# The first modulation in slabs of 4, 4, 4, 2, 2 tiles, and the late value products in three one-pass products

## The chip, the cores and the metric

The kernel runs on one core of a Trainium2 chip. The metric is the device time of one execution in microseconds (us), lower is better. Three runs of the kernel before gave 2869.8, 2873.56 and 2875.58 us; the median is 2873.56.

## The reference

Two transformer blocks run over one sequence of 512 tokens with 2048 features, all in float32. What matters here is how the first block begins:

```python
def first_block(x, c, norm_g, w_ada, b_ada, w_in, ...):
    cond = jax.nn.silu(c)
    mod = cond @ w_ada[l] + b_ada[l]                 # w_ada: 2048 x 6144
    shift, scale, gate = jnp.split(mod, 3, axis=-1)
    h = rms_norm(x, norm_g[l]) * (1.0 + scale[:, None, :]) + shift[:, None, :]
    z = h @ w_in[l]                                  # 2048 x 7184
    u_a, v_a, g_a, q_b, k_b, v_b, g_b, f_b = jnp.split(z, pts, axis=-1)
    y_a = chunked_spatial_gating(gelu(u_a), gelu(v_a), ln_v_g, ln_v_b, w_s, b_s) * silu(g_a)
    y_b = forgetting_attention(q_b, k_b, v_b, f_b, b_f[l]) * silu(g_b)
    ...
```

Before anything of `z` can be computed, `shift` and `scale` are needed, and these are a vector times 2048 x 4096 numbers of `w_ada` (33.5 MB). `v_a` (1024 columns) is the first product of `h`, `f_b` (the forget gates; 112 columns are taken) the second and `q_b` the third.

## The kernel before, in words

The features lie on the 128 partitions in KT = 16 tiles; `Y[:, t, :]` holds tile t of x, turned, with 512 tokens. Each engine has its own program, written out by hand; they meet in semaphores. There is no planner: the order within each program is the order of work.

**The start.** VectorE computes shift and scale in 4 slabs of 4 tiles. For a slab it goes through all 16 rows of tiles of `w_ada` (`accumulate`, L2431): a slice of 128 x (2 x 512) numbers, times the entry of c for its partition, is added to `acc`. SyncE loads these slices (L341, 512 KB each) into a ring of six, each as soon as the step that freed its place is counted in `acc_step`. TensorE then sums `acc` over the partitions (`reduce_slab`, L1689, 16 records of L1371), VectorE adds the bias and makes the columns of shift and scale (`slab_columns`, L2441 and L2443), modulates the four tiles (`slab_modulated`, L2460), and makes the low parts for later (`slab_low`, L2141, from the high parts that ScalarE makes in L1012). Before that it has multiplied the slab with the root of the norm (`slab_normed`, L2452). TensorE multiplies each modulated tile with the value weights in full float32, which takes four passes (`value_product`, L1704). These weights are loaded by GpSimd's queue (L616) into the four places of `w_raw`, each freed by `va_used`. Eight products belong to a tile: two groups of columns with four blocks of tokens each. Seven stay in their banks of PSUM over all slabs; for the eighth there is no bank, so after each slab VectorE adds it to a parked sum (`park`, L2475 and L2477) and its bank, number 7, also takes the sums of `reduce_slab`. TensorE does the sums of the next slab three products before the end of the present one.

**Behind it.** The groups f, q, k, v and so on (`GROUPS`) run in split precision: weights and operand are each cut in a high part (`w_hi` by ScalarE, L714 and L739; `op_hi`) and a low part (`w_lo` by VectorE, L2004; `op_lo`), and three one-pass products replace the four passes: high x high (L1414), low operand x high (L1417), high x low weights (L1420). `w_hi` and `w_lo` have four places, freed by `w_used`; the raw weights have four places of two tiles, freed by `lo_done`, and SyncE loads them (L383). f's tiles are 112 columns wide. While VectorE is free of the slabs it accumulates the next part of the modulation (`part_tile`, L2027); its loads for f's part are in L358.

**SyncE's order** after the slabs is: the f part of `w_ada`, b_f, the spill of x (L363, 4 MB from `Y` to HBM), b_s (L540), the eight weight pairs of f, the two rows ln_v_g and ln_v_b (L564), q's weights mixed with `a_raw`, the next part of `w_ada`. **ScalarE's order** is: the first two narrow high parts of f and two more, Gelu on the first four banks (L1032), Gelu on three banks and on the parked sum (L1035, L1037), then f's other high parts.

Of the kernel before, what the change touches and what calls it, by code (L numbers as in the profile page):

```python
# [5 lines left out]
P = 128  # L6
# [24 lines left out]
def plan():  # L31
# [36 lines left out]
    kc = 0  # L68
# [122 lines left out]
START_RING, SLABS, SLAB = 6, 4, 4  # L191
# [92 lines left out]
def va_block(b):  # L284

    slab, m = divmod(b, 4)
    return m % 2, SLAB * slab + 2 * (m // 2)


def value_order(slab):  # L290


    return (0, 1, 2, 3) if slab < SLABS - 1 else (0, 2, 1, 3)


# [29 lines left out]
def sync_program(B, sp):  # L325
# [24 lines left out]
    for m in range(KT // 2):  # L350
        n = SLABS * KT + m
        if m < START_RING:

            sp.wait_ge(sem("acc_step"), n - START_RING + 1)
        else:

            sp.wait_ge(sem("part_tile"), 2 * (m - START_RING) + 2)
# [4 lines left out]
    sp.wait_ge(sem("x_turned"), KT)  # L362
    sp.dma_start(B.x_sp, B.Y[:, :, :]).then_inc(sem("spilled"), 16)  # L363

    def weights(n, m, r=0):
# [3 lines left out]
        if g["kc"] + 2 * m < 2 * RAW:  # L369

            sp.wait_ge(sem("va_used"), 4 * (SLABS - 1) + value_order(SLABS - 1).index(m) + 1)
        if g["kc"] + 2 * m >= 2 * RAW:

            sp.wait_ge(sem("lo_done"), r * 8 + (g["kc"] + 2 * m - 2 * RAW + 2))
# [146 lines left out]
    def conv_loads(i, m):  # L521
# [7 lines left out]
        if 0 <= j < 8:  # L529
            if j >= CONV_SLOTS:  # L530
# [75 lines left out]

def pool_program(B, pool):
# [3 lines left out]
    for b in range(4 * SLABS):  # L611
        g, kt = va_block(b)
        if b >= RAW:
# [4 lines left out]
            .then_inc(B.va_in[b % RAW], 16)  # L618

# [80 lines left out]
def scalar_program(B, act):  # L700
# [5 lines left out]
    def high_tile(c, width):  # L706
        raw, fill = c // 2 % RAW, c // (2 * RAW)
        if c % 2 == 0:

            act.wait_ge(B.w_in[raw], 16 * (fill + 1))  # L710
# [1281 lines left out]
def vector_program(B, dve):  # L1992
# [519 lines left out]
    for t in range(SLAB):  # L2512
        slab_low(SLABS - 1, t)
# [496 lines left out]
```

## Time and profile before

| | |
|---|---|
| profiled execution | 2875.39 us, its span 2873.6 us |
| median of three runs | 2873.56 us |
| TensorE busy | 2788.6 us, 97% |
| VectorE busy | 1791.1 us, 62% |
| ScalarE busy | 1045.0 us, 36% |
| GpSimd busy | 43.1 us, 1% |
| DMA | 451.32 MB, 157 GB/s over the span |
| mean granted TensorE clock | 0.995 |

The span goes from the first to the last instruction; the time of the execution is 1.8 us longer. All times in what follows are microseconds from the span's start. A clock of 1.00 means that TensorE was granted its full 2.4 GHz throughout, and at the lower level it has 1.2 GHz. In the page's 40 slices of 71.8 us the DMA engines are at least 90% busy in the first two (digit 9), with 348 and 358 GB/s, and 60 to 70% in the next two, with 212 and 213 GB/s.

### The profile page before, as it was taken

How to read it: one execution, taken by the hardware profiler on the slowest of the kernel's cores; microseconds unless marked ns; L12 is line 12 of the kernel's file. 1: busy time of each engine (PE TensorE's matmuls, PEld its weight loads, DVE VectorE, ACT ScalarE, POOL GpSimd, SP SyncE). 2: the span in 40 equal slices, each digit the busy share in tenths (PEclk: the TensorE clock that was granted, in tenths of full speed). 3: DMA queues.
4: the chain of work that ended last, by engine and by line, in shares of the span. 5: the costliest groups of instructions: out<-in, count | busy, mean ns of one | idle time of the engine just before them, and what ended most of it. 6: DMA issues, size and time to landing. Idle time of an engine off the chain costs nothing.

```text
span 2873.6 us, 35430 instructions
## 1 busy us (share of the span) xinstructions
PE 2788.6 (97%) x12484; PEld 2203.0 (77%) x12484; DVE 1791.1 (62%) x2754; ACT 1045.0 (36%) x1636; POOL 43.1 (1%) x51
## 2 busy tenths in 40 slices
PE   7999999999999988999999999999999999999999
PEld 4468887777788866888877777777788688888887
DVE  6855675555598767445565647383977777525454
ACT  3032222444332365332243535443322542224233
POOL 0000000000000000000000000000000000100000
PEclk9999999999999999999999999999999999999999
DMA  9966553222356647465522223224667265333332
GB/s 348 358 212 213 190 191 95 75 74 80 120 191 220 237 145 234 151 216 192 189 89 81 82 87 102 73 88 141 217 228 220 89 234 191 106 99 96 124 111 96
DMA packets 239242, 451.32 MB, mean 157 GB/s; under 512 B 23918, under 2 KB 45888, under 8 KB 234482
## 3 DMA queue, kind: packets, MB, share of 16 engines
q1 hardware_dynamic: 236288, 440.85, 46.7%
q0 software_dynamic: 2304, 8.39, 0.8%
q8 instruction: 87, 1.43, 0.2%
q14 instruction: 59, 0.48, 0.1%
q10 hardware_dynamic: 504, 0.17, 0.0%
HBM read 422.06 MB, written 27.30 MB: 156 GB/s over the span
## 4 chain that ended last, share of the span: by engine, by line
PE 83%; DVE 6%; ACT 4%; issue 3%; DVEq 2%; DMA 1%; ACTq 1%; SPq 0%
PE ps L1414 20%; PE ps L1420 20%; PE ps L1417 19%; PE ps L1704 4%; PE ps L1433 2%; PE ps L1430 2%; PE ps L1427 2%; PE ps L1862 1%; PE ps L1853 1%; PE ps L1384 1%; PE ps L1981 1%; PE ps L1978 1%; PE ps L1389 1%; PE ps L1386 1%; PE ps L1352 1%
## 5 line engine op out<-in xcount | busy, mean ns | idle before, releaser
L2004 DVE TENSOR_TENSOR w_lo<-w_raw,w_hi 128x512 fp32r<-128x512 f32 (+2 forms) x672 | 448.7, 674 | 547.7 <-ACT w_hi L714 302.7
L1414 PE MATMUL ps<-op_hi,w_hi 128*128 128x512 f32 (+2 forms) x2800 | 779.3, 397 | 9.0 <-ACT w_hi L714 5.0
L1420 PE MATMUL ps<-op_hi,w_lo 128*128 128x512 f32 (+2 forms) x2800 | 755.3, 389 | 9.2 <-DVE w_lo L2004 4.7
L1417 PE MATMUL ps<-op_lo,w_hi 128*128 128x512 f32 (+2 forms) x2800 | 754.9, 389 | 0.6 <-DVE op_lo L2141 0.6
L1420 PEld LDWEIGHTS ps<-op_hi,w_lo 128*128 128x128 f32 (+1 forms) x2800 | 524.3, 188 | 123.5 <-DVE w_lo L2769 7.2
L1414 PEld LDWEIGHTS ps<-op_hi,w_hi 128*128 128x128 f32 (+1 forms) x2800 | 516.9, 188 | 125.7 <-issue 10.1
L1417 PEld LDWEIGHTS ps<-op_lo,w_hi 128*128 128x128 f32 (+1 forms) x2800 | 525.9, 188 | 112.7 <-DVE op_lo L2141 1.4
L714 ACT ACTIVATE w_hi<-w_raw 128x512 fp32r<-128x512 f32 (+2 forms) x416 | 242.7, 592 | 601.2 <-PE ps L1420 442.3
L739 ACT ACTIVATE w_hi<-w_raw 128x512 fp32r<-128x512 f32 x288 | 181.8, 632 | 583.6 <-PE ps L1420 454.1
L2027 DVE SCALAR_TENSOR_TENSOR acc<-a_raw,vec,acc 128x512 f32<-128x512 f32 x525 | 382.0, 747 | 16.2 <-DMA a_raw<-in_w_ada 13.6
L2769 DVE TENSOR_TENSOR w_lo<-w_raw,w_hi 128x512 fp32r<-128x512 f32 x128 | 83.6, 686 | 60.7 <-ACT w_hi L1270 55.3
L1427 PE MATMUL ps<-w_hi,op_hi 128*128 128x512 f32 x384 | 111.9, 400 | 5.3 <-ACT w_hi L714 4.4
L1433 PE MATMUL ps<-w_lo,op_hi 128*128 128x512 f32 x384 | 109.3, 393 | 3.5 <-DVE w_lo L2004 3.3
L1704 PE MATMUL ps<-w_raw,arena 128*128 128x512 f32 x256 | 111.7, 597 | 0.0
L1430 PE MATMUL ps<-w_hi,op_lo 128*128 128x512 f32 x384 | 108.9, 392 | 0.0
L1704 PEld LDWEIGHTS ps<-w_raw,arena 128*128 128x128 f32 x256 | 48.8, 192 | 61.0 <-issue 59.3
L2693 DVE TENSOR_TENSOR w_lo<-w_raw,w_hi 128x512 fp32r<-128x512 f32 x64 | 44.3, 692 | 76.3 <-ACT w_hi L1170 76.3
L1307 ACT ACTIVATE arena<-arena 128x2048 f32<-128x2048 f32 (+1 forms) x32 | 54.1, 1702 | 100.3 <-DVE arena L2825 100.3
L1427 PEld LDWEIGHTS ps<-w_hi,op_hi 128*128 128x128 f32 x384 | 71.5, 189 | 23.1 <-ACT w_hi L714 5.7
L1433 PEld LDWEIGHTS ps<-w_lo,op_hi 128*128 128x128 f32 x384 | 72.0, 189 | 21.4 <-DVE w_lo L2004 6.5
L1270 ACT ACTIVATE w_hi<-w_raw 128x512 fp32r<-128x512 f32 x128 | 74.8, 620 | 33.0 <-PE ps L1420 33.0
L1430 PEld LDWEIGHTS ps<-w_hi,op_lo 128*128 128x128 f32 x384 | 72.5, 189 | 15.5
(314 smaller groups left out, 2461.3 us busy)
## 6 DMA issues: line engine op xcount, KB each, us to landing
a_raw<-in_w_ada SPq DMA_DIRECT2D x216, 512.0 KB, 4.0
w_raw<-in_w_in_e SPq DMA_DIRECT2D x160, 512.0 KB, 4.7
w_raw<-in_w_in SPq DMA_DIRECT2D x96, 512.0 KB, 4.7
arena<-in_w_ada SPq DMA_DIRECT2D x72, 512.0 KB, 6.6
w_raw<-in_w_in_o SPq DMA_DIRECT2D x64, 512.0 KB, 4.4
w_raw<-in_w_out SPq DMA_DIRECT2D x32, 512.0 KB, 4.9
w_raw<-in_w_out_e SPq DMA_DIRECT2D x32, 512.0 KB, 5.0
w_raw<-in_w_out_o SPq DMA_DIRECT2D x32, 512.0 KB, 3.8
```

Of the source, the lines that this page charges most:

```text
L714: Act(B.w_hi[:, c % RING, 0:width], B.w_raw[:, raw, c % 2, 0:width], ACT.Copy).then_inc(sem("hi_done"), 1)
L739: Act(B.w_hi[:, t % RING, 0:width], B.w_raw[:, raw, t % 2, 0:width], ACT.Copy).then_inc(sem("hi_done"), 1)
L1414: mm(ps[0:m, bank + j, 0:tok], hi[:, cols], B.op_hi[:, k, 0:tok], start=first, stop=False)
L1417: mm(ps[0:m, bank + j, 0:tok], hi[:, j * P:j * P + m], B.op_lo[:, k, 0:tok], start=False, stop=False)
L1420: last = mm(ps[0:m, bank + j, 0:tok], lo[:, j * P:j * P + m], B.op_hi[:, k, 0:tok], start=False, stop=last_t)
L1427: mm(ps[:, bank + j, :], B.op_hi[:, k, rows], hi, start=first, stop=False)
L1430: mm(ps[:, bank + j, :], B.op_lo[:, k, j * P:j * P + P], hi, start=False, stop=False)
L1433: last = mm(ps[:, bank + j, :], B.op_hi[:, k, j * P:j * P + P], lo, start=False, stop=last_t)
L1704: return mm(ps[:, 4 * g + j, :], slab_input(B, slab)[:, t % SLAB, j * P:(j + 1) * P], B.w_raw[:, b % RAW, k, :], start=t % SLAB == 0 if ow ...
L2004: V.tensor_tensor(B.w_lo[:, c % RING, 0:width], B.w_raw[:, c // 2 % RAW, c % 2, 0:width], B.w_hi[:, c % RING, 0:width].bitcast(f32), ALU.s ...
L2027: last = V.scalar_tensor_tensor(out=sums, in0=x, scalar=col, in1=sums, op0=ALU.mult, op1=ALU.add)
L2769: V.tensor_tensor(B.w_lo[:, c % RING, :], B.w_raw[:, c // 2 % RAW, c % 2, :], B.w_hi[:, c % RING, :].bitcast(mybir.dt.float32), ALU.subtract)\
```

## The change

- `w_ada` is taken in 5 slabs of 4, 4, 4, 2 and 2 tiles. There are 80 accumulation steps instead of 64; the last 32 are half as wide. A load of the narrow slabs brings two rows of tiles into one place of the ring, in two DMAs of 256 KB.
- ScalarE instead of VectorE modulates the tiles (Identity with scale and bias) and makes the high parts of the operand beside it.
- The value products of the first two slabs stay as they were. From slab 2 on (`SPLIT_SLAB`) they are done as three one-pass products. ScalarE makes the high parts of the value weights and issues their loads (`value_high`, `value_load`), and GpSimd makes the low parts (`value_low`, a subtraction of 128 x 512 numbers, 16 of them).
- From slab 2 on the sums of the next slab stand directly behind the parked block's products of the last pair.
- VectorE normalises the next slab before it parks the last, and its low parts come one step earlier. The park of the last slab and the first two low parts of f's weights are put between the steps of f's part.
- The spill of x is issued by ScalarE's queue after the value activations. b_s is loaded behind f's weights. f's weights count on from the value products in the same rings.

The core of the diff:

```diff
-START_RING, SLABS, SLAB = 6, 4, 4
+START_RING, SLABS = 6, 5
+SLAB_AT, SLAB_TILES = (0, 4, 8, 12, 14), (4, 4, 4, 2, 2)
+SPLIT_SLAB = 2
...
+        for k in range(rows):
+            sp.dma_start(start_slot(B, n)[:, k, :, :], w_ada[:, kt + k, 0:2, first:first + width])\
+                .then_inc(B.start_in[n % START_RING], 16)
...
-    sp.wait_ge(sem("x_turned"), KT)
-    sp.dma_start(B.x_sp, B.Y[:, :, :]).then_inc(sem("spilled"), 16)
...
         if name == "f":
+            sp.wait_ge(sem("acc_step"), SLABS * KT)
+            sp.dma_start(at(AT_BS, 1, HEADS_A * P)[:, 0, :],
+                         A["b_s"].rearrange("o h t -> o (h t)").to_broadcast([P, HEADS_A * P])).then_inc(sem("bs_in"), 16)
             sp.wait_ge(sem("op_tile"), KT)
-            sp.wait_ge(sem("va_used"), 4 * SLABS)
+            sp.wait_ge(sem("w_used"), KT)
...
+def value_low(B, pool, b):
+    for c in (2 * (b - SPLIT_BLOCK), 2 * (b - SPLIT_BLOCK) + 1):
+        pool.wait_ge(B.sem("hi_done"), c + 1)
+        if c >= RING:
+            pool.wait_ge(B.sem("w_used"), c - RING + 1)
+        B.nc.gpsimd.tensor_tensor(B.w_lo[:, c % RING, :], B.w_raw[:, b % RAW, c % 2, :],
+                                  B.w_hi[:, c % RING, :].bitcast(mybir.dt.float32), mybir.AluOpType.subtract)
+        B.nc.gpsimd.drain().then_inc(B.sem("lo_done"), 1)
...
+        act.wait_ge(sem("columns_or_parked"), 2 * slab + 1)
+        for t in range(SLAB_TILES[slab]):
+            k = SLAB_AT[slab] + t
+            x, scale, bias = slab_input(B, slab)[:, t, :], B.mod[:, 16 + k:17 + k], B.mod[:, k:k + 1]
+            if slab >= SPLIT_SLAB:
+                Act(B.op_hi[:, k, :], x, ACT.Identity, scale=scale, bias=bias).then_inc(sem("op_high"), 1)
+                nc.scalar.drain()
+            Act(x, x, ACT.Identity, scale=scale, bias=bias).then_inc(sem("modulated"), 1)
...
+            if slab == SPLIT_SLAB:
+                value_load(SPLIT_BLOCK + RAW - 1)
+            for c in range(max(split, RING), split + 2 * SLAB_TILES[slab]):
+                if c % 2 == 0 and SPLIT_BLOCK + RAW + (c - RING) // 2 < KT:
+                    value_load(SPLIT_BLOCK + RAW + (c - RING) // 2)
+                value_high(c)
...
+                act.wait_ge(sem("columns_or_parked"), 2 * SLABS)
                 Act(va[:, 3, :], at(AT_PARK, S), ACT.Gelu).then_inc(B.bank_free[1], 1)
+                act.wait_ge(sem("x_turned"), KT)
+                act.dma_start(B.x_sp, B.Y[:, :, :]).then_inc(sem("spilled"), 16)
...
+    def split_products(slab, b, k, blocks):
+        g, kt = VA_BLOCKS[b]
+        t, c = kt + k, 2 * (b - SPLIT_BLOCK) + k
...
+        for j in blocks:
+            bank, first, last = value_bank(slab, g, t, j)
+            mm(bank, B.op_hi[:, t, rows(j)], hi, start=first, stop=False)
+        pe.wait_ge(sem("lo_done"), c + 1)
+        for j in blocks:
+            mm(value_bank(slab, g, t, j)[0], B.op_hi[:, t, rows(j)], lo, start=False, stop=False)
+        pe.wait_ge(sem("op_tile"), t + 1)
+        for j in blocks:
+            bank, first, last = value_bank(slab, g, t, j)
+            done = mm(bank, B.op_lo[:, t, rows(j)], hi, start=False, stop=last)
+        return done
...
     slab_columns(SLABS - 1)
-    slab_modulated(SLABS - 1)
-    for t in range(SLAB):
-        slab_low(SLABS - 1, t)
-
     for t in range(KT):
         part_tile(FIRST["f"], t)
-    park(SLABS - 1)
+        if t < SLAB_TILES[SLABS - 1]:
+            slab_low(SLABS - 1, t)
+        if t == 9:
+            park(SLABS - 1)
+        if t in (9, 11):
+            if t == 9:
+                dve.wait_ge(sem("lo_done"), KT)
+            low_tile(KT + (t - 9) // 2, GROUPS[FIRST["f"]]["width"])
```

## Rows read from the trace of the kernel before

**Rows 1.** Chain of waits over the start: start, length, engine, tile, line, records.
```profile
110.27 1.68 PE ps L1371 x16
111.95 27.57 PE ps L1704 x64
141.20 30.15 PE ps L1704 x70
...
176.19 7.79 DMA w_raw<-in_w_in
...
184.68 1.20 PE ps L1414 x4
185.88 0.91 PE ps L1417 x4
```

**Rows 2.** TensorE in order of time: start, length; idle before it at the end.
```profile
170.79 0.80 PE L1414 MATMUL ps<-op_hi,w_hi 128*112 128x512 f32 x1
...
182.20 1.02 PE L1358 MATMUL ps<-const 128*128 128x512 f32 x2
```

**Rows 3.** VectorE in order of time, one slab's end and f's part.
```profile
121.72 1.28 DVE L2431 SCALAR_TENSOR_TENSOR acc<-arena,vec,acc 128x1024 f32<-128x1024 f32 x1
122.91 0.69 DVE L2141 TENSOR_TENSOR op_lo<-arena,op_hi 128x512 fp32r<-128x512 f32 x1
...
125.31 11.00 DVE L2431 SCALAR_TENSOR_TENSOR acc<-arena,vec,acc 128x1024 f32<-128x1024 f32 x8
136.98 0.69 DVE L2477 TENSOR_TENSOR arena<-arena,ps 128x512 f32<-128x512 f32 x1 [0.67 <-PE ps L1704]
137.86 2.29 DVE L2452 TENSOR_TENSOR arena<-Y,arena 128x2048 f32<-128x2048 f32 x1 [0.19 <-issue]
...
146.56 12.72 DVE L2027 SCALAR_TENSOR_TENSOR acc<-arena,vec,acc 128x512 f32<-128x512 f32 x15
```

**Rows 4.** ScalarE in order of time: high parts of a slab, value activations.
```profile
142.31 2.19 ACT L1012 ACTIVATE op_hi<-arena 128x512 fp32r<-128x512 f32 x4 [26.02 <-DVE arena L2460]
...
171.39 1.45 ACT L1035 ACTIVATE arena<-ps 128x1536 f32<-128x1536 f32 x1 [0.75 <-PE ps L1704]
172.74 0.62 ACT L1037 ACTIVATE arena<-arena 128x512 f32<-128x512 f32 x1
```

**Rows 5.** GpSimd in order of time, late in the kernel.
```profile
2467.08 1.90 POOL L659 CAST gain_rows<-arena 128x2048 fp32r<-128x2048 f32 x1 [387.29 <-DVE Y L2940]
...
2474.99 4.61 POOL L663 TENSOR_TENSOR gain_rows<-arena,gain_rows 128x2048 fp32r<-128x2048 f32 x1
```

**Rows 6.** VectorE in order of time, the same stretch.
```profile
2467.17 2.34 DVE L2004 TENSOR_TENSOR w_lo<-w_raw,w_hi 128x512 fp32r<-128x512 f32 x1 [0.23 <-ACT w_hi L739]
...
2475.82 4.92 DVE L2004 TENSOR_TENSOR w_lo<-w_raw,w_hi 128x512 fp32r<-128x512 f32 x2 [0.73 <-ACT w_hi L739]
```

**Rows 7.** Busy time by stretch: length, PE, PEld, DVE, ACT, POOL, clock, DMA, GB/s.
```profile
26.40:28.60 2.20, 0.02 (x1) 0.00 (x0) 1.99 (x3) 2.20 (x3) 0.06 (x1) 1.00 1.04 386
28.60:32.00 3.40, 3.36 (x5) 1.48 (x6) 3.19 (x3) 1.78 (x1) 2.30 (x3) 0.64 1.05 387
32.00:36.00 4.00, 4.00 (x9) 1.66 (x8) 3.90 (x4) 1.86 (x1) 0.00 (x0) 0.88 1.04 390
```

**Rows 8.** DMA from 155 to 161 us, all packets.
```profile
DMA packets 80, 2.62 MB, mean 437 GB/s; under 512 B 0, under 2 KB 0, under 8 KB 0
```

**Rows 9.** DMA queues from 8 to 9 us: packets, MB, share of 16 engines.
```profile
q1 hardware_dynamic: 49, 0.40, 97.6%
q10 hardware_dynamic: 47, 0.02, 7.2%
```

**Rows 10.** DMA issues from 130 to 215 us: count, KB each, median to landing.
```profile
w_raw<-in_w_in SPq DMA_DIRECT2D x8, 112.0 KB, 2.4
...
arena<-in_ln_v_b SPq DMA_DIRECT2D x1, 512.0 KB, 5.8
```

**Rows 11.** SyncE's queue in order of time: start, length of the issue.
```profile
175.71 0.43 SPq L564 DMA_DIRECT2D arena<-in_ln_v_b  x1
```

More of the change, by code:

```diff
@@ L618, in pool_program @@
             .then_inc(B.va_in[b % RAW], 16)
+    for b in range(SPLIT_BLOCK, KT):
+        value_low(B, pool, b)
     queries = at(AT_QST, 2, S)
@@ L1692, in reduce_slab @@
         if slab:
-            pe.wait_ge(sem("parked"), slab)
+            pe.wait_ge(sem("columns_or_parked"), 2 * slab)
         else:
             pe.wait_ge(sem("variance"), 1)
-        reduce_parts(slab % 2, ps[:, 7, :]).then_inc(sem("start_summed"), 1)
+        tiles = SLAB_TILES[slab]
+        for v in range(2):
+            for j in range(tiles):
+                last = mm(ps[:, 7, tiles * v + j:tiles * v + j + 1], B.acc[:, slab % 2, v, j * P:(j + 1) * P],
+                          B.ones[:, 0:1], start=True, stop=True)
@@ L1698, in value_product, with value_bank @@
+        last.then_inc(sem("start_summed"), 1)
+    def value_bank(slab, g, t, j):
+        own = g == 1 and j == 3
+        first, last = (SLAB_AT[slab], SLAB_AT[slab] + SLAB_TILES[slab] - 1) if own else (0, KT - 1)
+        return ps[:, 4 * g + j, :], t == first, t == last
     def value_product(slab, b, k, j):
-        g, kt = va_block(b)
+        g, kt = VA_BLOCKS[b]
+        t = kt + k
         pe.wait_ge(B.va_in[b % RAW], 16 * (b // RAW + 1))
-        t = kt + k
-        own = g == 1 and j == 3
@@ L1704, in value_product @@
-        return mm(ps[:, 4 * g + j, :], slab_input(B, slab)[:, t % SLAB, j * P:(j + 1) * P],
-                  B.w_raw[:, b % RAW, k, :], start=t % SLAB == 0 if own else t == 0,
-                  stop=t % SLAB == SLAB - 1 if own else t == KT - 1)
+        pe.wait_ge(sem("modulated"), t + 1)
+        bank, first, last = value_bank(slab, g, t, j)
+        return mm(bank, slab_input(B, slab)[:, t - SLAB_AT[slab], j * P:(j + 1) * P],
+                  B.w_raw[:, b % RAW, k, :], start=first, stop=last)
@@ new lines, in split_products @@
+    def split_products(slab, b, k, blocks):
+        g, kt = VA_BLOCKS[b]
+        t, c = kt + k, 2 * (b - SPLIT_BLOCK) + k
+        hi, lo = B.w_hi[:, c % RING, :], B.w_lo[:, c % RING, :]
+        rows = lambda j: slice(j * P, (j + 1) * P)
+        pe.wait_ge(sem("hi_done"), c + 1)
+        pe.wait_ge(sem("op_high"), t + 1)
+        for j in blocks:
[6 more added lines that the diff above has]
+        for j in blocks:
+            bank, first, last = value_bank(slab, g, t, j)
+            done = mm(bank, B.op_lo[:, t, rows(j)], hi, start=False, stop=last)
+        return done
@@ L2527, in vector_program @@
     y_tile = lambda t: Y[:, t, :]
-    for c in range(4):
+    for c in (KT + 2, KT + 3):
         low_tile(c, GROUPS[FIRST["f"]]["width"])
```

188 lines of the change are left out of this document (113 added, 75 removed).

## The prediction

> **What bounds the kernel now.** I read the share of each engine first, then the chain of waits over the start, then TensorE, VectorE, ScalarE and SyncE in order of time there, then the transfers. TensorE is busy 97% of the span, so a change at the start is worth exactly what it moves TensorE's first product of q. The chain [rows 1] is TensorE alone through the value products: a wide slab is 32 four-pass products (64 records, two each) in 27.57 us, 0.862 us a product, and 1.68 us of sums, a period of 29.25. It ends with 30.15 us of products from 141.20, so the value products end at 171.35; I call this end V. Then 16 narrow tiles of f run from 170.8 to 182.2 [rows 2], one filling product 1 us long ends near 183.2, and q's first product starts at 184.68, because q's first weights, issued at 176.19, landed 7.79 us later [rows 1]. So q0 stands on a transfer, with V 13.3 us behind it. VectorE is the second limit: a chained 1024-wide accumulation costs 11.00/8 = 1.37 us, one with a short operation between 1.19, a low part 0.60, the normalising 2.29, a park 0.69, a chained 512-wide one 12.72/15 = 0.85 [rows 3].
>
> **Slabs 0 and 1.** The modulation leaves VectorE for ScalarE at 0.55 us a tile [rows 4], against 0.5 on VectorE, behind one semaphore. TensorE always has 3 products (2.6 us) left behind the sums, which hide it (without them it would be some 0.7 us a slab). Slab 2 starts as before: 111.95 + 3 x 0.862 = 114.5.
>
> **Three passes.** A one-pass product is 0.91/4 = 0.227 us [rows 1], three are 0.68 in place of 0.862. The 64 products of slabs 2 to 4 take 43.5 in place of 55.1 us: 11.6 less on TensorE if nothing is late; a k-tile is 2.72, slab 2 is 21.8, a narrow slab 10.9. Slab 2's park sum is done after 6.25 tiles' work, at 114.5 + 17.7 = 132.2. One more sum (5 slabs, narrow ones half of 1.68) adds nothing: 3 x 1.68 becomes 2 x 1.68 + 2 x 0.84.
>
> **VectorE, now 80 steps.** The last 32 are half as wide, but at 0.85 chained they cost 27.1 where 16 wide ones cost 22. In slab 3's loop, from the columns at 112.5: 10 x 0.85 + 4 x 0.67 + 4 x 0.60 = 13.6, and the two-tile normalising 1.2, done at 127.3: 4.9 us before the park sum at 132.2. Park, sums and columns follow: sums 133.1 to 134.0, columns 134.7. Slab 4's loop: 12 x 0.85 + 2 x 0.67 + 2 x 0.60 = 12.7, to 147.4, normalising 1.2, park 0.7: 149.4. TensorE had slab 3's park sum at 145.6 and now waits in order in front of the sums (in before it had 3 products there). So TensorE would idle 3.9 us, sum, do 18 passes (4.1), start slab 4 at 154.5 and end it 10.9 later: V = 165.4, 6.0 earlier, not 11.6.
>
> **The low parts on GpSimd.** No row shows this operation 512 wide beside an accumulation. The 2048-wide one takes 4.61 us [rows 5], so 1.15 for a quarter; the bounds are 0.69 (VectorE's time for it, [rows 3]) and 1.9 (a whole 2048-wide cast, [rows 5]). I take 1.15. TensorE has 2.72 us a tile, so by itself it is hidden. But what runs beside it pays: VectorE's subtraction of two SBUF tiles, 0.69 alone, took 2.34 and two took 4.92 while GpSimd worked [rows 5, 6]; the first waited until GpSimd was done (2467.08 + 1.90 = 2468.98, + 0.5 = 2469.5) and so did the other (2479.60). The accumulation too reads two SBUF tiles. Each GpSimd low part then holds VectorE for 1.15 less the gap of 0.15 between its instructions: 1.0 us (bounds 0, if accumulation does not collide, and 1.9). The first eight fall in VectorE's slack: four in slab 3's loop, which has 4.9 us, four in slab 2's, which has the 1.83 that the modulation leaves and its own waits (0.67 before the park, [rows 3]). If that cover were gone, each would cost 1.0 more. Four fall in slab 4's loop, which is on the path: + 4.0. The wait of GpSimd itself for VectorE delays TensorE's second passes by about 0.7 in slab 3 and 0.5 in slab 4. So: park 153.7, TensorE idle 146.2 to 153.8, sums to 154.7, 18 passes to 158.8, slab 4 with its waits 11.5: V = 170.3.
>
> **Clock.** After the 2.2 us idle at 26.4 the granted clock of the next 3.4 us was 0.64 [rows 7], that is 2.4 us at the lower level of 1.2 GHz; together with the 0.88 of the slice behind, 3.4 us, a loss of 1.7. With 7.6 us idle I charge 1.7 (bounds 0 and 3.5): V = 172.0, 0.7 later than before.
>
> **f.** Four accumulations more of the f part fall behind four further GpSimd low parts: VectorE is through its 16 f steps, park and two early low parts at about 175.6. The third narrow low part is ready at 175.9, where TensorE wants it at 173.8; f's fifth tile starts at 177.0 and f could end at 185.2.
>
> **The spill, now on ScalarE's queue.** It is issued after the value activations, 1.45 + 0.62 [rows 4] and a high part behind V: 174.7. In before it sat at 150, in front of f's weights on SP's own queue, under 20 us of TensorE work. Its cost there was nothing. It moves as 32 KB packets: 80 packets, 2.62 MB, at 437 GB/s [rows 8], so 9.7 us for 4.19 MB, 8 packets on each of 16 engines, 1.2 us each. How two queues share an engine stands in [rows 9]: in one microsecond q1 moved 49 packets of x and q10 47 of the small rows, one for one, while q1 had 97.6% of the time. So while the spill runs, SP's queue gets some 8 packets an engine. f's loads (256 rows of 448 bytes, 16 an engine) take 2.4 us alone [rows 10]; the last three pairs are issued at 176.2, 176.8 and 177.6, inside the spill (176.0 to 185.8), and land behind it. Their rest takes some 2.2 us: 188.0. Behind them in the same queue now stand b_s (moved here), both ln rows, and then q0. In before f's last pair landed near 177.1, the second ln row at 175.71 + 5.8 = 181.5 [rows 10, 11], so 2.2 a row, and q0 another 2.5 later, at 184.0. So three rows are 6.6: 194.6, and q0 197.1. With the high part of 0.7 TensorE starts q at 197.8.
>
> The Trainium skill has another rule here. "DMA: Bandwidth & Descriptors", section on queues, rings and completion order, says that an engine changes rings only at packet ends and that a packet typically holds 9 to 17 descriptors; by that f's loads would need one or two turns and lose about 2 us, which leads to the rival of a fair share below. Rows 9 speak against it.
>
> **Sum.** q starts at 197.8 in place of 184.7: + 13.1. TensorE was idle before it for over 5 us, so another clock loss of 1.7 (bounds 0 and 1.7): + 14.8; I take + 14.7, since the filling product covers a little. After q's first tile the work is the same and TensorE-bound, so it is not given back. Against the profiled execution's 2875.39 (span 2873.6 and 1.8 around) this is 2890.1. That execution is 1.8 above the median of 2873.56, so the forecast is 2888.
>
> **Rivals.** (1) Fair share: collision as above, but the queues share by bytes. SP's 2.4 MB (f's rest, b_s, ln, q0) at half of 400 GB/s take 12 us from 177, + 2: q0 at 191, q at 191.7, + 7.0: 2880.6. For: rows 9 have packets of 8 KB against small ones, no row has 32 KB beside another queue; against: the count there is one for one. (2) No collision on VectorE: V = 165.4, spill issued at 167.7, through at 178.8, f's rest 181, b_s and ln 187.6, q0 190.1, q 190.8, clock 1.7: + 7.8, 2881.4. Against it stand rows 5 and 6, which are of subtractions; for it, that no row has an accumulation there. (3) Not slower: TensorE's saved passes decide. No collision, V = 165.4, f ends 176.9, and SP's loads are not held up. q0, issued at 171.4 behind three broadcast rows, lands 3 x 2.2 + 2.5 = 9.1 us after f's last pair (169.7 + 2.4): 181.2, q 181.9, - 2.8: 2870.8; with the spill shared by bytes 183.7, - 1: 2872.5; with all cover 177.9, - 6.8: 2866.8. The point from which it decides: q0 lands before 184.0. (4) The narrow loads don't deliver: 1 KB rows halve the rate and slab 4's loop waits for data. 12 steps are in the ring, so 2 of 8 loads could be late, 3 us: this only widens the upper end.
>
> **Chances.** Forecast 0.58, rival 1 0.17, rival 2 0.11, rival 3 0.14. A measurement of this kernel tells 0.2%, 5.7 us, from no change (2867.8 to 2879.3). Faster: a third to a half of rival 3, 0.06. Same: the rest of it, and the lower part of 1 and 2 (spread 3 us), 0.15. Slower: 0.79. Range: rivals 1 and 2 lie inside; of rival 3 the milder half; above, GpSimd at 1.4 instead of 1.15 on 8 steps (2 us), the late loads (3) and a third clock drop (1.7): 2873 to 2896. The likeliest one's own range is 2882 to 2896.
>
> **What would show it.** Collision: accumulations in slab 4's loop near 1.9 us where GpSimd is busy, four of them or more; without it 0.75 at most. TensorE: idle before slab 4's sums, 7.6 us (3.9 without collision). V: 172 (165.4). Spill: f's last three pairs land about 10 us after issue in place of 2.4, TensorE idle within f, and q's first weights land 25 us after V, not 13. The forecast is wrong if q starts before 190; its mechanism is wrong if V comes before 168 or if f runs through without a wait.

## The result, and the profile after

The changed kernel takes 2886.7 us (median of five runs, 2882.76 to 2888.34); the kernel before 2872.97 (five runs, 2869.8 to 2875.58). The two medians are 13.7 us apart. The ratio on record is 1.0044, with a 95% interval of 1.0034 to 1.0055: slower by 0.44%, which is 12.6 us (9.8 to 15.8). Ratios leave out single executions of 6309 to 7573 us, of one changed kernel (y2_wide_split) and of the kernel before, which the medians keep; they move none of them by over 0.3 us. The forecast was 2888. The profiled execution of the changed kernel took 2886.70, its span 2884.9; TensorE is busy 2785.2 us in it against 2788.6, but its span less that busy time, the time in which it does nothing, is 99.7 us instead of 85.0. So the passes that the change takes out are gone, and more than that is lost in waiting and at a lower clock.

The chain of waits over the start of the changed kernel answers to [rows 1]; columns as there. Between the slabs it has left TensorE for VectorE, and in f it goes through a load.

```profile
112.50 2.68 PE ps L1800 x6
115.19 0.92 PE ps L1814 x4
...
139.49 1.80 DVE acc L2560
141.38 1.61 DVE acc L2560
...
151.75 1.75 DVEq L2586
153.58 0.69 DVE arena L2602
154.44 1.85 PE ps L1783 x8
156.79 0.81 ACT op_hi L1078
...
173.94 12.06 DMA w_raw<-in_w_in
186.02 0.30 ACT w_hi L747
186.37 0.49 PE ps L1498
...
188.08 0.43 PE ps L1498
...
193.74 0.86 PE ps L1442 x2
194.59 0.93 PE ps L1498 x4
```

TensorE in order of time, after (as [rows 2]): the idle stretches, each with what ended it, and the last value products.

```profile
133.79 1.02 PE L1783 MATMUL ps<-const,acc 128*128 128x1 f32 x8 [0.90 <-DVEq L2603]
154.44 1.84 PE L1783 MATMUL ps<-const,acc 128*128 128x1 f32 x8 [7.42 <-DVEq L2603]
172.59 0.84 PE L1821 MATMUL ps<-w_hi,op_lo 128*128 128x512 f32 x3
...
177.39 0.61 PE L1504 MATMUL ps<-op_hi,w_lo 128*112 128x512 f32 x1 [2.12 <-DVE w_lo L2128]
186.37 0.49 PE L1498 MATMUL ps<-op_hi,w_hi 128*112 128x512 f32 x1 [3.46 <-ACT w_hi L747]
```

The value products end at 172.59 + 0.84 = 173.43 (V), against 171.35 before. f, the narrow forget gates, runs from 173.3 to 193.7 instead of 170.8 to 182.2, and q's first product starts at 194.59 instead of 184.68: 9.9 later.

VectorE (as [rows 3]) and, behind it, GpSimd in order of time, after. The first VectorE row is the end of slab 4's loop, the second f's part.

```profile
139.49 12.88 DVE L2560 SCALAR_TENSOR_TENSOR acc<-arena,vec,acc 128x512 f32<-128x512 f32 x11
...
160.81 10.30 DVE L2151 SCALAR_TENSOR_TENSOR acc<-arena,vec,acc 128x512 f32<-128x512 f32 x8
```

```profile
139.38 1.35 POOL L633 TENSOR_TENSOR w_lo<-w_raw,w_hi 128x512 fp32r<-128x512 f32 x1 [11.07 <-ACT w_hi L1049]
140.97 1.46 POOL L633 TENSOR_TENSOR w_lo<-w_raw,w_hi 128x512 fp32r<-128x512 f32 x1 [0.24 <-ACT w_hi L1049]
142.67 1.47 POOL L633 TENSOR_TENSOR w_lo<-w_raw,w_hi 128x512 fp32r<-128x512 f32 x1 [0.24 <-issue]
144.37 1.46 POOL L633 TENSOR_TENSOR w_lo<-w_raw,w_hi 128x512 fp32r<-128x512 f32 x1 [0.24 <-issue]
```

Four of the eleven accumulations run beside a subtraction of GpSimd and start 1.7 to 1.9 apart (139.49, 141.38, 143.09, 144.79 in the chain), the others 0.85 apart. The starts of the two engines interleave with the same period: one waits for the other, in turn. Four more collide in f's part.

Granted clock and busy time by stretch, after (columns as [rows 7]):

```profile
150.00:154.40 4.40, 0.00 (x0) 0.00 (x0) 3.98 (x5) 0.00 (x0) 0.00 (x0) 0.53 0.78 254
154.40:157.00 2.60, 2.56 (x10) 2.50 (x11) 0.48 (x3) 0.21 (x1) 0.00 (x0) 0.50 0.58 206
157.00:160.00 3.00, 3.00 (x8) 2.32 (x8) 1.68 (x3) 2.84 (x4) 0.00 (x0) 0.50 0.02 5
160.00:165.00 5.00, 5.00 (x22) 4.05 (x22) 4.59 (x4) 2.30 (x5) 3.82 (x3) 0.95 0.35 105
177.00:180.00 3.00, 2.61 (x7) 1.86 (x8) 1.44 (x7) 0.59 (x2) 0.00 (x0) 0.60 0.85 354
180.00:183.00 3.00, 2.91 (x11) 1.87 (x9) 0.00 (x0) 0.00 (x0) 0.00 (x0) 0.83 0.84 354
187.00:190.00 3.00, 3.00 (x10) 2.17 (x9) 0.95 (x4) 0.89 (x3) 0.00 (x0) 0.64 1.03 391
190.00:193.00 3.00, 3.00 (x12) 2.25 (x11) 0.34 (x2) 0.75 (x2) 0.00 (x0) 0.79 1.03 394
```

After the 7.42 of idle TensorE works for 5.6 us at 1.2 GHz, a granted clock of 0.50, and some of the next five at 0.95: 5.6 x 0.5 + 5 x 0.05, about 3.0 us lost (an estimate from these rows). Twice more, after 2.12 and after 3.46 of idle in f, passes take 0.43 instead of 0.23 (the chain has one at 188.08).

ScalarE's queue, the issues of transfers from 130 to 215 us (as [rows 10]) and the packets of both DMA queues from 176 to 177 and from 178 to 179 us (as [rows 9]), after:

```profile
173.48 0.35 ACTq L1121 DMA_DIRECT2D x_spill<-Y  x1
173.67 1.44 ACT L1117 ACTIVATE arena<-ps 128x1536 f32<-128x1536 f32 x1
```

```profile
x_spill<-Y ACTq DMA_DIRECT2D x1, 4096.0 KB, 12.2
...
arena<-in_w_ada SPq DMA_DIRECT2D x8, 256.0 KB, 3.1
...
w_raw<-in_w_in SPq DMA_DIRECT2D x8, 112.0 KB, 5.3
arena<-in_b_s SPq DMA_DIRECT2D x1, 512.0 KB, 7.9
arena<-in_ln_v_g SPq DMA_DIRECT2D x1, 512.0 KB, 7.7
arena<-in_ln_v_b SPq DMA_DIRECT2D x1, 512.0 KB, 7.3
```

```profile
q10 hardware_dynamic: 16, 0.52, 123.3%
...
q10 hardware_dynamic: 16, 0.52, 124.3%
q1 hardware_dynamic: 16, 0.01, 2.5%
```

The spill (q10) leaves at 173.48. In its first microseconds it has the engines to itself; then SyncE's queue (q1, f's weights) gets one packet of some 450 bytes for each packet of 32 KB. f's last four pairs, issued from 173.9 to 179.9, land from 186.0 to 187.1, 7.2 to 12.1 after their issue.

### The profile page after: what moved, and what is told of

It reads as the page before. It is cut to its first block, busy times and chain, and to the rows that moved or that the text cites. A ratio compares the mean times of both kernels' runs of the same rounds, so it can differ in the third digit from the quotient of the medians.

```text
span 2884.9 us, 35769 instructions
## 1 busy us (share of the span) xinstructions
PE 2785.2 (97%) x12548; PEld 2218.9 (77%) x12548; DVE 1801.0 (62%) x2758; ACT 1068.4 (37%) x1668; POOL 62.8 (2%) x59
## 4 chain that ended last, share of the span: by engine, by line
PE 81%; DVE 7%; ACT 3%; issue 3%; DMA 2%; DVEq 2%; ACTq 1%; SPq 1%
PE ps L1498 20%; PE ps L1504 20%; PE ps L1501 19%; PE ps L1517 2%; PE ps L1511 2%; PE ps L1514 2%; PE ps L1800 2%; PE ps L1986 1%; PE ps L1977 1%; PE ps L1468 1%; PE ps L2102 1%; PE ps L2105 1%; PE ps L1473 1%; PE ps L1470 1%; DVE acc L2151 1%
## 5 line engine op out<-in xcount | busy, mean ns | idle before, releaser
L1504 PE MATMUL ps<-op_hi,w_lo 128*128 128x512 f32 (+2 forms) x2800 | 757.3, 390 | 11.3 <-DVE w_lo L2128 6.9
L2560 DVE SCALAR_TENSOR_TENSOR acc<-arena,vec,acc 128x1024 f32<-128x1024 f32 (+1 forms) x75 | 89.8, 1197 | 13.7 <-DMA arena<-in_w_ada 7.2
L2976 DVE TENSOR_TENSOR arena<-arena,Y 128x2048 f32<-128x2048 f32 (+1 forms) x32 | 64.4, 2024 | 16.1 <-ACT arena L1391 15.6
```

What stands on the lines that cost most here:

```text
L1504: last = mm(ps[0:m, bank + j, 0:tok], lo[:, j * P:j * P + m], B.op_hi[:, k, 0:tok], start=False, stop=last_t)
L2560: last = V.scalar_tensor_tensor(out=sums, in0=x, scalar=col, in1=sums, op0=ALU.mult, op1=ALU.add)
```

## The experiments

Ten kernels were run, in three groups, each beside the kernel before (medians there: x 2873.3, y 2873.7, z 2872.9; x and y on one chip, z on another). In the table S is the start of the column sums ahead of slab 2, V the end of the last value product, q the start of q's first; these and the span are of the one profiled execution, the median is of all runs.

| kernel | S | V | q | q less S | span | median | ratio to before, 95% |
|---|---|---|---|---|---|---|---|
| before | 110.11 | 171.35 | 184.68 | 74.57 | 2873.6 | 2872.97 |  |
| changed | 110.65 | 173.43 | 194.59 | 83.94 | 2884.9 | 2886.7 | 1.0044 (1.0034 to 1.0055) |
| x1_small_packets | 109.26 | 172.03 | 194.30 | 85.04 | 2883.9 | 2884.41 | 1.0042 (1.0028 to 1.0056) |
| x2_spill_early | 110.36 | 173.31 | 189.40 | 79.04 | 2880.9 | 2880.21 | 1.0021 (1.0008 to 1.0034) |
| x3_quiet_gpsimd | 108.56 | 167.48 | 187.82 | 79.26 | 2878.4 | 2878.34 | 1.0016 (1.0007 to 1.0026) |
| x4_before_late_spill | 108.73 | 169.97 | 192.34 | 83.61 | 2879.9 | 2882.09 | 1.0026 (1.0010 to 1.0042) |
| y1_both_causes | 110.20 | 169.63 | 185.01 | 74.81 | 2871.0 | 2875.78 | 1.0006 (0.9997 to 1.0015) |
| y2_wide_split | 109.11 | 165.48 | 182.94 | 73.83 | 2873.4 | 2870.23 | 0.9990 (0.9982 to 0.9999) |
| y3_sums_late | 109.53 | 174.36 | 194.05 | 84.52 | 2886.1 | 2887.49 | 1.0052 (1.0037 to 1.0067) |
| z1_rows_behind_q | 110.28 | 165.41 | 179.19 | 68.91 | 2865.9 | 2868.69 | 0.9983 (0.9974 to 0.9992) |
| z2_gpsimd_lows | 108.64 | 170.12 | 186.23 | 77.59 | 2878.4 | 2877.49 | 1.0011 (1.0001 to 1.0020) |
| z3_spill_late | 111.14 | 167.79 | 188.11 | 76.97 | 2872.4 | 2874.21 | 1.0003 (0.9994 to 1.0012) |

Span less q is 2684.3 (z3) to 2692.2 (z2): the work behind q's start is the same, and it differs by up to 8 us between profiled executions. So q tells what an edit did at the start, and only medians say what it was worth. And a ratio need not be that of two medians: x4's medians are 8.8 us apart, and its ratio is 7.4 us, with an interval of 2.9 to 12.1.

**The start differs too.** S goes from 108.56 to 111.14, and the edits have no part in it: the sums of the slab ahead start 29.25 to 29.30 before S in every kernel, at 79.3 to 81.9, before anything that the ten edits touch. The kernel before and x4 do the same work up to there. TensorE's sums in before and in x4, and its busy time and granted clock from 53 to 60 us in both:

```profile
110.11 1.84 PE L1371 MATMUL ps<-const,acc 128*128 128x1 f32 x16
...
108.73 1.84 PE L1371 MATMUL ps<-const,acc 128*128 128x1 f32 x16
```

```profile
53.00:60.00 7.00, 7.00 (x17) 3.20 (x17) 6.63 (x11) 2.19 (x4) 0.00 (x0) 0.76 0.86 280
...
53.00:60.00 7.00, 6.84 (x19) 3.06 (x19) 6.63 (x11) 2.19 (x4) 0.00 (x0) 1.00 0.85 285
```

In these 7 us x1, x3, x4, y2 and z2 had the full clock; before, the changed kernel, x2, y1 and z1 had 0.76, y3 0.79 and z3 0.56. The order of these clocks is the order of S: 108.56 to 109.26 at the full clock, 109.53 at 0.79, 110.11 to 110.65 at 0.76 and 111.14 at 0.56. So V and q of two kernels are compared from S on: q less S in the table, and V less S in the text.

**x1_small_packets.**

```diff
-        self.x_sp = nc.dram_tensor("x_spill", (P, KT, S), ...).ap()
+        self.x_sp = nc.dram_tensor("x_spill", (P, KT, 2 * S), ...).ap()[:, :, 0:S]
```

> The changed kernel with one edit: the spilled copy of x has its rows of 512 numbers 4 KB apart in HBM, so the same 4 MB, issued at the same place on ScalarE's queue, goes as 2048 packets of 2 KB in place of 128 of 32 KB. Theory (engines serve the two queues packet by packet, whatever the size): f's last three weight pairs, which land 8 to 12 us after issue in the changed kernel, land within 5 us, and the 3.5 us in which TensorE waits inside f is gone. The bytes in front of q's first weights are the same 6.6 MB, so q starts only 2 to 3 us earlier, near 192, and the time is 2 to 3 us under the changed kernel's 2886.7 (2884). Rival (the queues share by bytes, the delay is the amount of data): the pairs still land 8 us or more after issue, and the time stays within 1 us.

The wait of 3.46 in f is gone (0.22 and 0.76 are left) and f's pairs land in a median of 4.0 instead of 5.3. But q's pair comes no sooner, against the 2 to 3 us expected: the same bytes lie ahead of it. TensorE in order of time in x1, q's first products:

```profile
194.30 2.08 PE L1498 MATMUL ps<-op_hi,w_hi 128*128 128x512 f32 x4 [4.55 <-ACT w_hi L747]
```

The wait has moved from f to q, and behind it q's passes take 0.43 instead of 0.23 (the granted clock is 0.66 from 190 to 200 us). So the length of the packet turns explains f's wait. That the bytes hold q fits, and rests on x2 as well. The median is 2.3 lower, as expected, but the ratios (1.0042 and 1.0044) are not told apart.

**x2_spill_early.** The changed kernel, the spill issued at 138.9 instead of 173.5:

```diff
+            if slab == 3:
+                act.wait_ge(sem("x_turned"), KT)
+                act.dma_start(B.x_sp, B.Y[:, :, :]).then_inc(sem("spilled"), 16)
```

> The changed kernel with the spill moved on ScalarE's queue to behind the high parts of slab 3, near 141 us, where SyncE's queue has six loads in hand. Theory (the late spill holds up f's weights and q's): f's pairs land in 2.4 to 3.5 us, no wait of TensorE inside f, f ends near 188.5, q's first weights come 9 us after f's last pair, near 187.5, and q starts near 189.5 in place of 194.6: 5 us under the changed kernel, 2881.5. The value products still end near 173.3, so it stays 6 to 9 us above the kernel before. Rival (the loss comes from the value products alone, the spill is hidden behind waits that are there anyway): 2886, no change within 1 us. A third case: the early spill starves the loads of the f part of w_ada, VectorE waits, and the value activations or f's low parts come later, 2886 to 2890.

f's pairs land in 2.6, of f's waits only the low part's 2.0 is left, q starts 5.2 earlier (4.9 from S on), and the median falls by 6.5. V and the idle before slab 4's sums (7.4) stay.

**x3_quiet_gpsimd.** The low parts of the value weights are left out.

```diff
-        B.nc.gpsimd.tensor_tensor(B.w_lo[...], B.w_raw[...], B.w_hi[...], subtract)
+        B.nc.gpsimd.memset(B.w_lo[:, c % RING, :].bitcast(f32), 0.0)
```

> The changed kernel with GpSimd's subtraction replaced by a memset of the same tile, which reads nothing; so the low parts of the value weights are left out of the result, all instructions of TensorE stay. Theory (VectorE is held while GpSimd reads SBUF): the accumulations of slab 4's loop go at 0.85 us a step instead of 1.7, the wait of TensorE ahead of slab 4's sums shrinks from 7.4 to about 4, the value products end near 169.5 in place of 173.3, and the third narrow low part of f is in time (2.1 us less waiting); f is then held by the spill as before. In all 4 to 6 us under the changed kernel: 2881 to 2883. Rival (a memset takes the port as well, or the steps are slow for their narrow shape): steps stay at 1.7 where GpSimd works, or at 1.2 with its shorter 0.53 us, and the time within 2 us of 2886.7.

VectorE in order of time in x3: eleven accumulations in 9.30, where the changed kernel needs 12.88. GpSimd still works beside them, 0.53 us for each memset, but only writes, and none of them is held:

```profile
137.39 9.30 DVE L2559 SCALAR_TENSOR_TENSOR acc<-arena,vec,acc 128x512 f32<-128x512 f32 x11
```

That is (12.88 - 9.30) / 4 = 0.90 for each subtraction. V is 6.0 earlier, but S is 2.1 earlier already. So the edit is worth 3.9 at V, close to four times 0.90 and to the 3.8 that was expected. The idle before slab 4's sums is 4.4 instead of 7.4. The late spill then bites harder: TensorE waits 5.4 in the midst of f. The median falls by 8.4, where 4 to 6 was expected; the ratios give 8 with some 4 either way, so this is not settled. That a subtraction collides and a memset does not is what the Trainium skill says in "SBUF — State Buffer", section "Who interferes with whom": a VectorE instruction with two SBUF inputs meets a GpSimd instruction that reads SBUF, and not one that only writes it. This trace agrees, with 1.7 against 0.85 a step.

**x4_before_late_spill.** The kernel before with the spill alone moved to where the change has it.

```diff
-    sp.wait_ge(sem("x_turned"), KT)
-    sp.dma_start(B.x_sp, B.Y[:, :, :]).then_inc(sem("spilled"), 16)
...
                 Act(va[:, 3, :], at(AT_PARK, S), ACT.Gelu).then_inc(B.bank_free[1], 1)
+                act.wait_ge(sem("x_turned"), KT)
+                act.dma_start(B.x_sp, B.Y[:, :, :]).then_inc(sem("spilled"), 16)
```

> The kernel before with one edit: the spill of x goes from SyncE's queue at 150 us to ScalarE's queue behind the value activations, as in the changed kernel; b_s stays early. Theory (packet by packet): the spill runs from about 173 to 183, f's last three pairs land behind it, TensorE waits some 3 us or more inside f and runs part of it at the lower clock, the two ln rows and q's first weights follow, and q starts near 191 in place of 184.7: 6 us above the kernel before, 2879. Rival (fair share by bytes): f is hardly held, q's first weights come 2 to 3 us later, 2875 to 2876. Rival (all hidden): 2873.

The late spill alone, with no other part of the change, costs 8.8 us by the medians (2882.09 against 2873.3). It puts q 7.7 later, and 9.0 later from S on. Both are more than the 6 us expected. In f TensorE waits 8.8 at one place, where some 3 or more was expected. TensorE's longest wait in x4, of those from 100 to 200 us:

```profile
PE ps L1414 <- ACT w_hi L712: 8.8, 1, 8.8
```

**y1_both_causes.** The edits of x2 and x3 together (low parts of the value weights left out).

```diff
-        B.nc.gpsimd.tensor_tensor(B.w_lo[...], B.w_raw[...], B.w_hi[...], subtract)
+        B.nc.gpsimd.memset(B.w_lo[:, c % RING, :].bitcast(f32), 0.0)
...
+            if slab == 3:
+                act.wait_ge(sem("x_turned"), KT)
+                act.dma_start(B.x_sp, B.Y[:, :, :]).then_inc(sem("spilled"), 16)
```

> The changed kernel with both earlier edits together: the spill is issued by ScalarE's queue behind the third slab's high parts, and GpSimd writes zeros in place of the sixteen subtractions (so the low parts of the value weights are left out of the computation). Alone the first edit gave 2880.2 and the second 2878.3, against 2886.7. If the two costs are separate ones that add (the spill between f's pairs and q0; the collision, the idle of TensorE and the lower clock before it), their gains add, 6.5 and 8.4: 2886.7 - 14.9 = 2871.8, with q's first product at 183 to 185 and no wait inside f over 1 us. If they overlap (with an earlier end of the value products f's pairs are asked for earlier, and q0 then waits for the broadcast rows, which follow VectorE's own end), the time is 2875 to 2878, with q's start at 186 or later and a wait for q's pair or for the reciprocal norm just before it.

2875.8, 10.9 below the changed kernel and 4 above the sum of the two gains. The time is as expected of the second theory, q's start (185.0) as of the first. From S on q comes 9.1 earlier than in the changed kernel, and the two edits alone give 4.9 and 4.7: at q the two costs add. The 4 us that the medians lack are within the intervals of the three ratios. Two waits have come in the place of the old ones, as TensorE's waits in y1 show. f's first product now stands behind the table load and the activation of the value part, because f's first pair came late and ScalarE takes its high part first; and q stands behind its own pair.

```profile
PE ps L1498 <- ACT w_hi L746: 2.0, 1, 2.0
PE ps L1498 <- ACT arena L1114: 1.0, 1, 1.0
```

The early spill has a price of its own here: VectorE waits 2.94 for its first load of f's part. Of the 13.7 us that the change costs, these two causes hold about 11; with both gone no difference to before can be measured (ratio 1.0006, 0.9997 to 1.0015).

**y3_sums_late.** The changed kernel with the sums of the next slab behind all products of the slab before.

```diff
-                    if slab >= SPLIT_SLAB and slab < SLABS - 1:
-                        reduce_slab(slab + 1)
...
+            if b == final and slab >= SPLIT_SLAB and slab < SLABS - 1:
+                reduce_slab(slab + 1)
```

> The changed kernel with one thing moved: in the split slabs the column sums of the next slab stand behind all three-pass products of the slab before rather than inside them, so that the eighteen passes or so that followed the sums now come ahead of them and fill the time in which VectorE is not done with its steps. If TensorE's 7.4 us of idle before slab 4's sums is what makes its clock fall afterwards, the idle is 3 to 4 us, the clock falls less, and slab 4's products start 1 to 3 us earlier: 2883 to 2885. If the end is set by VectorE's chain alone (steps, sums, normalising, park), the idle shrinks but slab 4 starts no earlier, the same waits show behind the sums, and the time stays 2886 to 2888.

No gain: V less S is 64.8 where it was 62.8. TensorE's waits in y3 from 100 to 200 us:

```profile
PE ps L1814 <- ACT w_hi L1049: 8.8, 2, 4.4
...
PE ps L1783 <- DVEq L2603: 2.3, 1, 2.3
```

The idle before the sums is 2.3, but it comes back as 4.4 behind them, twice, while ScalarE modulates: nothing is left to fill it. Slab 4's first product comes 52.0 behind S, against 51.7 in the changed kernel. The rival held: the chain through VectorE, sums and modulation sets slab 4's start, and the idle is where it shows, not what makes it.

**y2_wide_split.** The useful part of the change in another arrangement, nothing left out. The edit is against the changed kernel; it also has the other twelve low parts on VectorE, the moved order of park and normalising, and b_s ahead of f's weights.

```diff
-SLAB_AT, SLAB_TILES = (0, 4, 8, 12, 14), (4, 4, 4, 2, 2)
+SLAB_AT, SLAB_TILES = (0, 4, 8, 12), (4, 4, 4, 4)
...
-    for b in range(SPLIT_BLOCK, KT):
-        value_low(B, pool, b)
...
+            if slab == SPLIT_SLAB + 1 and kt in (7, 8, 10, 12):
+                value_low_here(4 + (7, 8, 10, 12).index(kt))
...
+            if slab == SPLIT_SLAB + 1:
+                act.wait_ge(sem("x_turned"), KT)
+                act.dma_start(B.x_sp, B.Y[:, :, :]).then_inc(sem("spilled"), 16)
```

> Nothing left out. The first modulation in four slabs of four tiles as before, but the products of the third and fourth in three passes as after; all low parts of the value weights by VectorE, none by GpSimd; the fourth slab's column sums behind all products of the third; its loads and first four high parts ahead of the column scaling; the spill on ScalarE's queue in the middle of the fourth slab's modulation; the broadcast of b_s ahead of f's weights. If the cost of the change lay in the two narrow slabs (a second normalising and park), GpSimd's collision and the late spill, this ends the value products at about 164 (170.3 before) and starts q at 176 to 178: 2864 to 2868. If VectorE's sixteen added subtractions (0.5 to 0.6 each, some 9 us) and the wide park fall between slab 3's products and slab 4's, TensorE waits there over 6 us, the value products end at 168 to 171, and the time is 2870 to 2875. Slower than 2876 if the spill now stands in ScalarE's activations or in f's weights.

`value_low_here` is VectorE's subtraction, and the last three lines issue the spill behind the modulation of the fourth slab. V is 165.5, 5.9 before the kernel before (4.9 from S on), near what was expected; q came at 182.9 and not at 176 to 178, because f starts 3.4 behind V (the same activation as in y1), does its first passes at the lower clock, and q's pair, behind two broadcast rows, lands at 182.3. The median is 2870.2: 0.1% faster by a ratio whose interval just misses 1.

**z1_rows_behind_q.** y2_wide_split with the three rows moved behind q's fourth pair (the lines that go are not shown):

```diff
+            if n == FIRST["q"] and m == 3:
+                for r, v in enumerate(("ln_v_g", "ln_v_b")):
+                    sp.dma_start(at(TMP, 2, 1024)[:, r, :], ...)
+                sp.dma_start(at(AT_BS, 1, HEADS_A * P)[:, 0, :], ...)
```

> Nothing left out. The four wide slabs of the run before (y2_wide_split), with the three broadcast rows (two of the value norm, and b_s) no longer ahead of q's first pair but behind its fourth on SyncE's queue. In y2_wide_split q's first pair was asked for at 175.6 behind the two rows, landed 6.7 us later, and q started at 182.9 with TensorE filling 1.6 us before it. If the rows stood between f's pairs and q0, q0 lands 2 to 2.6 us earlier (1 MB at some 390 GB/s), f starts as before, and q is then held only by the end of f's products, about 181.4 and one high and one low part: q at 181.5 to 182, 2868.5 to 2869.5. If what holds q is the end of f, its time is that of y2_wide_split, 2870, and q's start moves by under 0.5 us.

q starts at 179.2, 2.3 earlier than expected (4.9 earlier than in y2 from S on): with b_s gone from before f's weights as well, f starts at 167.1 after 1.67 of idle and keeps the full clock, and nothing waits for q's pair. 2868.7, ratio 0.9983: the lowest median of all, though its interval overlaps that of y2. It beats the kernel before by 0.17% and, by the medians, the changed one by 0.6%.

**z2_gpsimd_lows.** y2_wide_split with `value_low` on GpSimd and none on VectorE.

```diff
+    for b in range(SPLIT_BLOCK, KT):
+        value_low(B, pool, b)
...
-            if slab == SPLIT_SLAB + 1 and kt in (7, 8, 10, 12):
-                value_low_here(4 + (7, 8, 10, 12).index(kt))
```

> Nothing left out. y2_wide_split with the sixteen low parts of the value weights subtracted by GpSimd, as in the changed kernel, and none by VectorE. In the changed kernel each subtraction held VectorE's steps up by 0.85 us. If it is the same place by place, VectorE loses 0.85 where it gives back 0.5 to 0.7 of its own: the end of the value products moves from 165.2 to between 165 and 169, and the time is 2870 to 2874. If the collision costs only in narrow slabs, where VectorE's work comes twice in short stretches, the value products end before 165 and the time is under 2869.5.

Worse than either theory: 2877.5, V 4.6 later than in y2 (5.1 from S on). VectorE in order of time in z2:

```profile
120.61 19.41 DVE L2564 SCALAR_TENSOR_TENSOR acc<-arena,vec,acc 128x1024 f32<-128x1024 f32 x9
```

That is 2.16 a step on average, where three chained ones take 4.06 in y2 (1.35). The nine lose 7.3; in the same stretch y2 has four subtractions of its own at 0.6 and two waits for loads (1.35 and 0.67) that z2 does not have, so z2's last step ends 2.7 later, at 140.0. The rest, 1.9 of V's 4.6, is TensorE's: it idles 5.2 before the last sums, and its granted clock is 0.55 from 140 to 145 and 0.50 from 145 to 150, against 0.67 and 0.99 in y2. In the changed kernel half of the sixteen subtractions fell in slack; here seven and the end of an eighth fall in these nine steps.

**z3_spill_late.** y2_wide_split with the spill behind the value activations.

```diff
-            if slab == SPLIT_SLAB + 1:
-                act.wait_ge(sem("x_turned"), KT)
-                act.dma_start(B.x_sp, B.Y[:, :, :]).then_inc(sem("spilled"), 16)
...
                 Act(va[:, 3, :], at(AT_PARK, S), ACT.Gelu).then_inc(B.bank_free[1], 1)
+                act.wait_ge(sem("x_turned"), KT)
+                act.dma_start(B.x_sp, B.Y[:, :, :]).then_inc(sem("spilled"), 16)
```

> Nothing left out. y2_wide_split with the spill on ScalarE's queue where the changed kernel has it, behind the last high parts. In the kernel before the late place cost 9.2 us of median (2873.3 to 2882.1) and moved q by 7.7; in the changed kernel 6.5. If it is the bytes and the packet turns between f's pairs and q0, it costs here as much: spill issued at about 163 to 165, f's pairs after the fourth land 8 us or more after their issue, q starts at 188 to 191, and the time is 2876 to 2879. If y2_wide_split's early spill only moved the wait to slab 4's loads and f's first pairs (which landed 10.8 us after their issue), the late one costs under 2 us: 2870 to 2872.

q is at 188.1 as the first theory has it, 5.2 later than in y2, with 6.0 of waiting in f. But 2.0 of the 5.2 stand there at S already, with the clock of 0.56 ahead of it, so that the late place is worth 3.1 at q (76.97 against 73.83); and the median is 4.0 higher and not 6 to 9. So the late spill costs in every arrangement: 8.8, 6.5 and 4.0 by the medians, 9.0, 4.9 and 3.1 at q from S on. It costs less where q is held by other things anyway; that is a reading of these three pairs, and no run varies it alone.

## Why the prediction was right

**Slab 2's start** was put at 114.5 and is 115.19. 0.5 of the difference is there before slab 2: its sums come at 110.81 and not at 110.27 [rows 1], with the same granted clock of 0.76 from 53 to 60 us in both. The forecast had three products left behind the sums in every slab, which would hide ScalarE's modulation. In slab 0 there are none, and TensorE waits 0.50 for the first modulated tile, as TensorE in order of time after shows; in slabs 1 and 2 it does not wait, as said.

```profile
54.76 26.80 PE L1800 MATMUL ps<-w_raw,arena 128*128 128x512 f32 x58 [0.50 <-ACT arena L1080]
```

The working says 6.25 tiles ahead of slab 2's park sum, but the 17.7 us that it adds are 6.5 tiles, and so are the 18 passes left behind the sums; the time was right.

**VectorE and the collision.** The idle before slab 4's sums was forecast as 7.6 with the collision and 3.9 without; it is 7.42, and 4.4 in x3. Each subtraction holds an accumulation 0.85 to 0.90 and not 1.0; the subtraction itself takes 1.35 to 1.47, not 1.15. That the accumulation collides at all was inferred from subtractions [rows 5, 6] and is shown by x3, where it is worth 3.9 at V; the forecast priced it at 4.9 with GpSimd's own waits (170.3 against 165.4). Rival 2 falls.

**V** came at 173.4 instead of 172.0. The clock is the term that was mis-sized: 1.7 charged, about 3.0 lost. Of the 1.4 by which V is late these 1.3 are the largest term; 0.6 at the start of slab 4's sums (154.44, forecast 153.8) and 0.5 less in slab 4 itself (11.0, forecast 11.5) nearly cancel. ScalarE's modulation also was mis-sized: 0.81 for the tile (156.79 in the chain) and as much for its high part, one behind the other, where 0.55 was taken from another activation [rows 4]; what that alone costs no run separates.

**f.** The third low part was to be 2.1 late, at 175.9; TensorE, by then 1.4 later itself, waits 2.12 for it, until 177.39.

**The spill.** It was to be issued at 174.7 and to run from 176.0 to 185.8 at 437 GB/s; it leaves at 173.48 and lands 12.2 later, at 185.7. A packet takes 1.23 us (16 packets fill 123.3% of 16 engines for one microsecond), so it runs at some 425 GB/s, close to the forecast. Its queue had to wait only for the semaphores in front of it, and not for the activation ahead of it, which starts at 173.67. One for one was right: 16 packets of 32 KB and 16 small ones in one microsecond. The rule of the Trainium skill ("DMA: Bandwidth & Descriptors", queues, rings and completion order), with typically 9 to 17 descriptors to a turn, would let f's weights through in one or two turns; that is an estimate, and takes a packet of the profile for one descriptor. This trace does not agree: they waited 7 to 12 us, and rival 1 falls with it. f's last pair landed at 187.1, forecast 188.0.

**q's first pair** was the largest error: forecast 197.1, landed at 192.54, 5.4 behind f's last pair and not 9.1. Three rows at 2.2 each and q0 at 2.5 were laid end to end, while they overlap: the four are issued within 6.1 us, and the rows land in 7.3 to 7.9 each, q0 in 5.7. Another thing was missing on the other side: f runs partly at the lower clock and ends at 193.57, so q, at 194.59, is held as much by f as by its pair, 3.2 before the forecast.

**The sum.** q was to start 13.1 later, with 1.6 of clock: + 14.7 on the profiled execution of before. That execution became longer by 11.3 (2875.39 to 2886.70), 9.9 of it at q's start. The 1.6 of clock was charged to q after 5 us of idle. That idle did not come: TensorE waited 3.46 within f, the lower clock fell on f's passes, and q's first passes take 0.23. The 1.4 behind q is within what the rest of the program differs by itself. Against the medians the change cost 13.7 and not 11.3, because the profiled execution of before lay 2.4 above the median of five (1.8 above that of the three known then) and that of after on its own. So that forecast and result are only 1.3 us apart is in good part luck: the mechanism, its places and its order are shown, and the term for q was 3 too large. Rival 3, not slower, would need both causes gone, and y1, where they are, is level with before. Rival 4 did not occur: the narrow loads land in 3.1.

## What to carry to other kernels

A big transfer costs nothing only where its place in time is covered. Moved by some 20 us to the point where small, urgent loads begin, the same 4 MB cost 4 to 9 us in three kernels, first by packet turns and then by its bytes; before moving a transfer, look at what is issued within its length behind it. GpSimd, though it looks idle, is no free help where its instruction reads SBUF and VectorE's critical one reads two tiles there: it did sixteen subtractions worth 0.6 each, and VectorE lost 0.85 to 0.9 on each that fell beside a chain of accumulations. A profile that differs from another by 2 us at q may have differed by 2 us before the edit: find the last place that both have alike, here S, and count from there. And halved slabs do not halve a chain's cost per step: compare [rows 3], 0.85 for half the width of 1.37.

## What was unexpected of the hardware

- The clock does not follow idle time in a simple way. After 7.42, 3.46 and 2.12 us of idle TensorE worked at the lower level for some time; after 1.67 (z1) it did not. The same work from 53 to 60 us was granted 0.76 in the kernel before and 1.00 in x4. And the same idle of 2.2 at 26.4 us, after which the kernel before fell to 0.64 [rows 7], left the changed kernel at 1.00, with other work around it:

```profile
26.40:28.60 2.20, 0.29 (x3) 0.05 (x1) 1.99 (x3) 2.20 (x4) 0.00 (x0) 1.00 1.05 387
28.60:32.00 3.40, 3.12 (x8) 1.45 (x9) 3.19 (x3) 2.01 (x2) 2.36 (x3) 1.00 1.05 386
```

- A short window overstates the rate of large packets: 16 of 32 KB in one microsecond read as 524 GB/s, and the share of 123.3% beside it tells that they took 1.23 us each, some 425 GB/s. Over 6 us of the spill before it was 437 [rows 8]. Loads at their densest move 394 (the last row of the clock windows).
- With packets of 2 KB (x1) the spill takes 14.4 us instead of 12.2 to land, and f's pairs 4.0 instead of 5.3.
- Where VectorE and GpSimd both take two SBUF inputs, they go by turns: 1.61 and 1.46 long, at a period of 1.70, so GpSimd's 128x512 subtraction took from 1.27 to 3.06 us depending on what VectorE did (the longest beside the normalising).
